# One attention kernel, one engine swap: ScalarE instead of VectorE multiplies the attention weights by the reciprocal row sums

## The reference, cut to what matters

```
s = einsum(q, k) * scale + bias            # -inf where masked
m = max(s);  p = exp(s - m)
p = p / (sum(p) + exp(sink - m))           # the causal ones have no sink
o = einsum(p, v)
```

## Time and profile before

| | |
|---|---|
| median of 3 runs | 2168.18 us (2167.18 to 2173.62) |
| profiled execution, its own time | 2170.31 us |
| its span, first to last instruction | 2168.5 us |
| busy: TensorE, VectorE, ScalarE, GpSimd | 90%, 55%, 35%, 15% |
| attention stage 1 | about 157 to 325 us |
| attention stage 2 | about 1520 to 1725 us |
| granted TensorE clock, mean | 0.96 of full speed |

### The profile page before, as it was taken

How to read it: one execution, slowest core, us unless ns; L and a number is a source line. 1 busy time by engine, 2 the same in 40 slices (tenths; PEclk the granted TensorE clock), 3 DMA queues, 4 the chain that set the end, 5 groups by cost and what they waited for, 6 DMA issues and landing times.

```text
span 2168.5 us, 22425 instructions
## 1 busy us (share of the span) xinstructions
PE 1957.2 (90%) x9050; PEld 1610.0 (74%) x9050; DVE 1189.5 (55%) x1857; ACT 753.6 (35%) x1132; POOL 327.2 (15%) x288
## 2 busy tenths in 40 slices
PE   2159999999999998999899999989988889999996
PEld 1148878877888887887688888767877667888885
DVE  6026655656676755555765545475565474333436
ACT  3036553234232224222422222264555343222223
POOL 2023321012111112001300000056222040000002
PEclk9679999999999999999999999989999889999998
DMA  8532216635665631542354532213111123232321
GB/s 264 65 90 78 79 54 234 222 108 211 215 214 192 225 126 60 196 153 97 128 204 174 194 116 97 97 58 122 40 40 40 59 61 109 85 99 94 97 97 39
DMA packets 126072, 267.49 MB, mean 123 GB/s; under 512 B 4431, under 2 KB 33119, under 8 KB 125968
## 3 DMA queue, kind: packets, MB, share of 16 engines
q1 hardware_dynamic: 121008, 248.53, 34.5%
q0 software_dynamic: 4960, 17.53, 2.3%
HBM read 257.65 MB, written 8.39 MB: 123 GB/s over the span
## 4 chain that ended last, share of the span: by engine, by line
PE 76%; DVE 10%; ACT 6%; another core or an unknown queue 3%; issue 2%; POOL 2%; DMA 1%; SPq 0%; ACTq 0%; POOLq 0%; DVEq 0%
PE ps L582 23%; PE ps L584 23%; PE ps L583 23%; DVE t L1526 2%; DVE t L1578 1%; ACT t L1132 1%; DVE t L1560 1%; PE ps L695 1%; DVE t L1517 1%; DVE t L1500 1%; DVE t L1514 1%; ACT t L1164 1%; PE ps L677 1%; PE ps L678 1%
## 5 line engine op out<-in xcount | busy, mean ns | idle before, releaser
L582 PE MATMUL ps<-t 128*128 128x512 f32 (+1 forms) x2584 | 1006.8, 390 | 102.9 <-DVE t L1531 68.3
L584 PE MATMUL ps<-t 128*128 128x512 f32 (+1 forms) x2584 | 998.0, 386 | 0.0
L583 PE MATMUL ps<-t 128*128 128x512 f32 (+1 forms) x2584 | 997.6, 386 | 0.0
L582 PEld LDWEIGHTS ps<-t 128*128 128x128 f32 x2584 | 489.5, 189 | 209.3 <-DVE t L1409 73.1
L584 PEld LDWEIGHTS ps<-t 128*128 128x128 f32 x2584 | 488.9, 189 | 103.4
L1409 DVE TENSOR_TENSOR t<-t 128x2048 fp32r<-128x2048 f32 x135 | 310.2, 2298 | 463.5 <-ACT t L1039 463.5
L583 PEld LDWEIGHTS ps<-t 128*128 128x128 f32 x2584 | 489.5, 189 | 98.0 <-issue 1.0
L1039 ACT ACTIVATE t<-t 128x2048 fp32r<-128x2048 f32 x135 | 258.1, 1912 | 615.7 <-PE ps L584 611.7
L1418 DVE CUSTOM_DVE_ANT_0 t<-t 128x1024 f32<-128x1024 f32 x160 | 198.5, 1283 | 20.3 <-DMA t<-in_ada_t 12.5
L1463 DVE SCALAR_TENSOR_TENSOR t<-ps,t 128x512 f32<-128x512 f32 x184 | 132.4, 748 | 83.7 <-PE ps L584 75.1
L1526 DVE TENSOR_TENSOR t<-ps,t 64x512 fp32r<-64x512 f32 (+4 forms) x183 | 102.9, 577 | 134.1 <-ACT t L1164 58.2
(11 more groups left out here) (150 smaller groups left out, 1426.1 us busy)
## 6 DMA issues: line engine op xcount, KB each, us to landing
t<-in_ada SPq DMA_DIRECT2D x48, 1024.0 KB, 6.0
t<-in_gate SPq DMA_DIRECT2D x22, 1024.0 KB, 5.1
t<-in_up SPq DMA_DIRECT2D x22, 1024.0 KB, 5.1
t<-in_down SPq DMA_DIRECT2D x22, 1024.0 KB, 5.0
t<-in_w_in SPq DMA_DIRECT2D x17, 1024.0 KB, 5.7
t<-in_w_mlp_in SPq DMA_DIRECT2D x16, 1024.0 KB, 5.5
t<-in_w_mlp_out SPq DMA_DIRECT2D x16, 1024.0 KB, 5.1
t<-in_ada_t POOLq DMA_DIRECT2D x13, 1024.0 KB, 5.6
```

What stands on the lines that cost most here:

```text
L582: pe.matmul(o, wh, xh, start=first, stop=False)
L583: pe.matmul(o, wh, xl, start=False, stop=False)
L584: return pe.matmul(o, wl, xh, start=False, stop=last)
```

## The change

ScalarE multiplies all four pieces, in the order 0, 1, 2, 3. VectorE keeps only the reciprocal. The transposes wait for ScalarE's semaphore for every piece.

```diff
@@ transposes (TensorE)
-                    if i == 3:
-                        on.wait_ge(a_exp, "scaled", st, h, 3)
-                    else:
-                        on.wait_ge(d_soft, "scaled", st, h, i)
+                    on.wait_ge(a_exp, "scaled", st, h, i)
@@ ScalarE, step "norm"
                         on.wait_ge(a_exp, "exp", st, h, 3)
                         on.wait_ge(d_soft, "recip", st, h)
-                        act.activation(prob(st, h, 3), prob(st, h, 3), ACT.Copy, scale=stats(h)[4][:, 3:4]).then_inc(
-                            a_exp.sem, a_exp.up("scaled", st, h, 3))
+                        for i in range(4):
+                            act.activation(prob(st, h, i), prob(st, h, i), ACT.Copy, scale=stats(h)[4][:, i:i + 1]).then_inc(
+                                a_exp.sem, a_exp.up("scaled", st, h, i))
@@ VectorE, normalise
                 dve.reciprocal(rs, sm).then_inc(d_soft.sem, d_soft.up("recip", st, h))
-                on.wait_ge(d_soft, "recip", st, h)
-                for i in range(3):
-                    dve.tensor_scalar(prob(st, h, i), prob(st, h, i), rs[:, i:i + 1], 1.0, ALU.mult, ALU.mult).then_inc(
-                        d_soft.sem, d_soft.up("scaled", st, h, i))
```

## The result

| | before | changed |
|---|---|---|
| median | 2169.12 us (6 runs) | 2182.62 us (6 runs) |
| lowest to highest | 2166.63 to 2176.34 | 2180.82 to 2185.05 |
| profiled execution, its span | 2168.5 us | 2183.2 us |

The ratio is 1.0057 with a 95% interval of 1.004 to 1.0074, which is 8.7 to 16.1 us: the changed kernel is slower, by 13.5 us if one goes by the medians. The forecast was 2180, 11.8 above before.

What follows compares the result with a forecast made beforehand. TensorE bounds the kernel, with stalls from latency between VectorE's and ScalarE's queues. Terms -4.5 + 9.8 + 2.4 + 2.6 + 1.5 = +11.8 us took the profiled 2170.3 to 2182.1, stated as 2180 against the median; range 2171 to 2187.

Steps and rivals of the forecast that it cites:

- The price on ScalarE: Three additional multiplications per causal head on ScalarE, ahead of t2's rounding: 1.22 us, bounds 0.86 and 1.5.
- The blocked heads: Nine causal heads where VectorE's multiplications are slow beside GpSimd: 0.39 us gained in eight, 1.4 in one, together -4.5 us.
- The free heads: Eight causal heads where t0 follows VectorE's L1526 within 0.1 us: each pays the full 1.22 us, +9.8 us.
- The three with slack: Free heads 2.3, 2.7 and 2.11, where t0 starts some time after the low half of t2: +2.4 us together.
- Edges and swa heads: Heads 1.8, 1.9, 2.0, 2.1 between kinds of heads: +2.6 us; eight swa heads, next exponential later: +1.5 us.
- The clock: TensorE granted 1.2 GHz for a few us behind some stalls: nothing in the sum, -2 to +3 us in the range.
- Rival A: Port lock counts in full, blocked heads regain 20 us: 2148, 5 in 100; milder form 2164; 6 in 100 together.
- Rival B: No difference: price nearer 0.86 us or half the delays vanish in TensorE's slack, +3 to +6 us; 20 in 100.
- Rival C: Slower by more: swa heads pay 0.5 us each and three more clock dips come, +17.6 us, 2186; 19 in 100.

Runs made afterwards that it cites:

- e1: Kernel before, with ScalarE multiplying all four pieces only in the nine heads where VectorE was held up beside GpSimd; 2158.44 us, ratio 0.9953.
- e2: Kernel before, with ScalarE multiplying all four pieces in 23 heads, the nine where GpSimd held up VectorE left as before; 2193.28 us, ratio 1.0114.
- e8: Kernel before, with ScalarE multiplying all four pieces only in the eight swa heads (1.0 to 1.7); 2169.65 us, ratio 1.0004.
- e3: Probe: kernel before, with GpSimd's pieces in the attention stages cut from 512 to 16 columns, the rest left out; 2144.31 us, ratio 0.9887.
- e5: Changed kernel, with the previous head's t2 rounding put ahead of ScalarE's four multiplications in 22 causal heads; 2162.99 us, ratio 0.9967 to before.
- e7: Kernel before, with ScalarE multiplying all four pieces only in the nine held-up heads, and t2's rounding put ahead of the multiplications; 2150.22 us, ratio 0.9914.
- e6: Kernel before, with only the rounding of the previous head's t2 put ahead of the multiplication in ScalarE's queue; 2169.68 us, ratio 1.0006.

## Why the prediction was right

**The price on ScalarE.** Taken as 386, 496 and 606 ns less three overlaps, 1.22 us. Measured, ScalarE's groups by form in the changed kernel:

```profile
L1154 ACT ACTIVATE t<-t 128x256 f32<-128x256 f32 x48 | 22.2, 494 | 0.0
...
L1154 ACT ACTIVATE t<-t 128x384 f32<-128x384 f32 x24 | 14.4, 601 | 0.0
L1154 ACT ACTIVATE t<-t 128x128 f32<-128x128 f32 x32 | 12.6, 394 | 14.7 <-DVE t L1573 14.7
```

The four take 1.91 us, 1.20 more than the one did. The bounds from PSUM copies (0.86) and without overlap (1.5) were not needed. The formula of the Trainium skill, page "ScalarE: Activation LUTs", section "What ACT_TABLE_LOAD costs" (280 ns and 0.833 ns per column where one operand is a pointer), gives 387, 493 and 600 ns; the trace agrees within 2%.

**The blocked heads.** Nine, as read from the earlier trace rows. I expected a path of 2.87 us; it is 2.69 in all nine, since from L1156 to the rounding it was 259.30 - 258.69 = 0.61 us there and 0.75 in the free head, and I had taken the free one's path for both. So the gain was 0.59 in eight and 1.6 in one, 6.3 us by the paths instead of 4.5, and 9.2 us in e1's runs. The term was too small by a third to a half, on the safe side of the sign.

**The free heads.** Expected +1.22 each in eight, measured 1.19 to 1.20 by the path. The three with slack: +2.4 expected, and 0.70, 0.90 and 0.90 = 2.5 us by the same paths. VectorE's 0.88 us was no cover: the paths grew by the whole price, here and in e2.

**Edges and swa heads.** +1.5 for the swa heads against 2 us of later matmuls and 1.5 us of time in e8. The edges came to about 3.2 us against 2.6, by how much later t0 starts from head to head in the two traces.

**The clock.** Set at nothing in the sum, with -2 to +3 in the range. In the profiled execution it is most of the 4 us between the stages. In the experiments it went along with the stalls: e1 gained 3 us more than its paths (9.2 against 6.3), e3 6 us more (23.3 against 17), and e2 lost 8 us more (25.7 against 9.6 + 2.5 for the free heads and 3.2 + 2 for edges and swa heads). That is the term that was thought of too small: the granted clock went up where stalls shrank in e1 and e3, and down where they grew in e2. In the change itself, where some stalls shrink and others grow, it comes to about +2 by the estimate in the last section, inside the range that was given.

**What was luck.** The mechanism and the price stood, but the two halves of the sum were both too small and partly made up for each other: the blocked heads were put at -4.5 and the rest at +16.3, and e1 and e2 measured -9.2 and +25.7. That the total, 13.5, came out within 2 us of 11.8 owes something to that.

**The rivals.** Rival A, the lock counting in full, is refuted by the result and by e1 (9.2 us and not 20), and e3 shows what it would have taken: VectorE's multiplications free of GpSimd, with nothing put on ScalarE in their place, 23 us. Rival B (at most +6) lies below the interval, which begins at +8.7. Rival C, +17.6, is just outside it, which ends at +16.1.

VectorE is held up by GpSimd's instruction (2.99 against 0.88 us in e3), and ScalarE is not (1.91 us beside GpSimd, 1.92 without, in the changed kernel). The rule of the Trainium skill on the shared port pair ("SBUF — State Buffer", section "Who interferes with whom") agrees with both; that the cause is a lock on ports no run here shows. By that rule alone the move would have paid. What decided was what stood behind the moved work in ScalarE's queue.

## What to carry to other kernels

When work moves to an engine that is only a third busy, look at what stands directly behind it in that engine's queue. Here three more multiplications, 1.2 us, stood ahead of one 0.39 us rounding in each head, and putting the rounding first made the changed kernel some 19 us faster. It did not make the multiplications free: in the heads where VectorE was not held up they still cost 12.8 us (e5 against e7). A stall that comes and goes with another engine's activity should be fixed where it happens (e1, e7), and not everywhere.

## What the runs showed that was not expected

The time moved by more than the paths did, in both directions. TensorE's busy time for the same 1020 matmuls of stage 2 was 163 us at a mean granted clock of 0.97 in e1, 170 at 0.94 before and 174 at 0.92 in e2:

```profile
1529.00:1740.00 211.00, 173.81 (x1025) 154.52 (x1024) 106.42 (x302) 115.16 (x284) 39.19 (x37) 0.92 0.11 36
```

The repeated runs show it too. The table has the mean granted clock of each kernel's runs, less that of the runs of the kernel before timed beside them; the estimate of what it is worth, at 1.73 us for 0.001 and before rounding; what is left of the measured difference; and what the paths of the traces add up to, where that was worked out. For the changed kernel the clock of its own neighbours is not on record, and the mean of the other rounds, 0.9606, stands in.

| kernel | clock | measured, us | of it clock (estimate) | left | paths |
|---|---|---|---|---|---|
| e1 | +0.0021 | -9.2 | -3.6 | -5.6 | -6.3 |
| e2 | -0.0036 | +25.7 | +6.2 | +19.5 | +17.3 |
| e3 | +0.0039 | -23.3 | -6.8 | -16.5 | -17 |
| changed | -0.0013 | +13.5 | +2.2 | +11.3 | |
| e6 | -0.0021 | +1.6 | +3.6 | -2.1 | |
| e7 | +0.0027 | -17.9 | -4.8 | -13.1 | |

With the clock taken out, e1 and e3 lie within 1 us of their paths and e2 within 2.2, and the changed kernel lies within 1 us of the forecast's +11.8, which had the clock at nothing. Shortening a stall can thus pay twice. It need not: e6 shortened stalls and was granted less. What decides which stall is followed by the lower level was not settled: the earlier trace rows already had two stalls of like length, one with it and one without.
